# A decoder block with gated recurrence and windowed attention: the attention's two key blocks folded into one block of 128 scores, masks applied behind the turn by VectorE

## The chip, the cores and the metric

One Trainium2 chip (trn2), one of its cores. The metric is the device time of one launch in microseconds (us). The kernel before ran three times: 2208.53 us median, 2208.11 to 2211.46.

## The reference, cut to what matters

One decoder block over 2048 tokens of width 1024: an RMS norm, one input projection, two mixers side by side (a gated linear recurrence with 4 heads, and attention with 8 query heads of 64 on 2 key heads), one output projection, a gated feed-forward part and a last norm. The change lies in the attention:

```python
kk = with_prev(kb)            # keys of the block before and of this block: 256
vv = with_prev(vb)
scores = einsum('bnqhgd,bnshd->bhngqs', qb, kk) * (B_HEAD_DIM ** -0.5)
dist = qi + BLOCK - kj        # 128 queries against 256 keys
valid = ((dist >= 0) & (dist < WINDOW)) & (key_pos >= 0)
scores = where(valid, scores - slopes * dist, -inf)
m = maximum(max(scores), sink)
p = exp(scores - m)
p = p / (sum(p) + exp(sink - m))
o = einsum('bnhgqs,bnshd->bnqhgd', p, vv)
```

WINDOW and BLOCK are both 128. So of the 256 keys beside a query exactly 128 are valid: with query row q and key column k of a block, the key k of this block is valid for k <= q, and the key k of the block before for k > q. The two valid parts fill one 128x128 square without overlap.

## The kernel before, in words

The 2048 tokens go in four blocks (`it`, 0 to 3) of 512. For each block a function `slots(it)` stands in every engine's program, with 27 slots (line 67), and behind it `out_b(it)`; behind all four blocks the feed-forward part (`ffn`, `down`) takes the rest of the time, from about 900 us on. Every engine has its own program and waits for the others by semaphores; the order within an engine is the order in which the code issues.

A slot of TensorE begins with one group: 24 matmuls that make 128 columns of the input projection (`group`, lines 939 to 948). Behind it stand short pieces of the mixers. The attention has 16 steps in a block (4 pairs of heads, `p`, times 4 token tiles, `b`), one per slot, and each step passes through the slots as line 69 says: scores of step i in slot i + 2, probabilities in slot i + 3, the turn in slot i + 4, the product with the values in slot i + 5. Slots 4 to 19 thus hold a turn. In one slot TensorE does, in this order: the group, the turn of a head's output if there is one (line 1083), scores, the turn of the probabilities, the value product, and then the recurrence's pieces.

One step, for two heads (a pair) and 128 queries:

- TensorE (`scores`, line 997): per head two matmuls into 256 columns of bank X[0], which hold the scores against the keys of the tile before and of this tile.
- VectorE (`scores`, lines 1752 to 1763): per head one addition over 256 columns, X[0] plus the slope times a table of distances (`dist`, with a large negative number where a key is not valid; `dist0` for the first tile), into `pr`; one max reduce over 2x256; two small operations for the negative maximum and the sink.
- ScalarE (`scores`, lines 1335 and 1337): two exponentials of 256 columns with their sums, and one for the sink.
- VectorE (`denominators`, lines 1733 and 1737): sum and reciprocal, as the first thing in its next slot.
- GpSimd (`normalise`, line 2306): one product of 128x512 with the two reciprocals. In one step per block it also copies `dist` over `dist0` (line 2311).
- TensorE (`p_turn`, line 1009): four transposes of 128x128 into bank X[1]. It waits for `s_pT` of the step before (line 1005), since the bank is single.
- ScalarE (`p_turn`, line 1343): copies X[1] to `pT`, as the first of the three attention pieces in its slot.
- TensorE (`pv`, line 1020): per head two products of 128 keys with the values, accumulated in M[3].

VectorE's slot (`slots`, from line 1866) holds, in order: the denominators; the low half of the weights for two slots ahead (`make_lo`, line 1704), which waits for ScalarE's high half `whi`, and that for TensorE's group of this slot; the turned head's gate; the low halves of the queries; `scores`; the eviction of four finished value products (line 1899); the head's piece (`head_group`: a scan, gated queries, reciprocals); then `keys` (line 1805), `update` (line 1823, eight in a chain) and `head_sum` (lines 1833 and 1835); and last, in slots 12 to 15 of blocks 1 to 3, the scaling of a row of h (`h_scale`, line 2030).

Before the blocks, GpSimd prepares the tables (lines 2248 to 2278), and TensorE, ScalarE and VectorE wait for its counts INI and DST (line 513).

## Time and profile before

| | |
|---|---|
| median of three runs | 2208.53 us |
| lowest, highest | 2208.11, 2211.46 us |
| the profiled execution | 2210.02 us |
| its span | 2208.3 us |
| mean granted TensorE clock | 0.998 of full speed |
| instructions | 29323 |
| busy: TensorE, VectorE, ScalarE, GpSimd | 2162.4, 1428.7, 1001.3, 455.5 us |

The span is the time from the first to the last instruction of the profiled execution. Names in the profile: PE is TensorE's matmuls, PEld its weight loads, DVE VectorE, ACT ScalarE, POOL GpSimd. L12 is line 12 of the kernel. In a timeline a row gives the start in us, the length in us, engine, line, operation, output and inputs, and how many like it are merged; in square brackets the idle time before it and what ended that.

### The profile page before, as it was taken

The page shows a single profiled execution, that of the slowest core. Times are in us where ns is not written, and L with a number is a line of the kernel's source. Part 1 is how long each engine was busy: PE and PEld are TensorE (multiplying, and loading weights), DVE is VectorE, ACT ScalarE, POOL GpSimd, SP SyncE. Part 2 cuts the span into 40 slices and gives each one's busy share as a digit, 9 for nine tenths or more (in the row PEclk, how much of TensorE's full clock was granted, in tenths as well). Part 3 has the DMA queues.
Part 4 walks back from the last instruction along what each step waited for, and adds up shares of the span by engine and source line. Part 5 has one row for each costly group of instructions (what it writes and reads, how often), then busy time and mean ns, then how long its engine had stood idle before and what let it go on. Part 6 is the DMA issues. An engine that isn't in the chain of part 4 may idle for free.

```text
span 2208.3 us, 29323 instructions
## 1 busy us (share of the span) xinstructions
PE 2162.4 (98%) x10792; PEld 1788.9 (81%) x10792; DVE 1428.7 (65%) x2142; ACT 1001.3 (45%) x1809; POOL 455.5 (21%) x344
## 2 busy tenths in 40 slices
PE   7999999999999999999999999999999999999997
PEld 6887887888888888778888887888888888887886
DVE  5776578657865786867466675568655555554555
ACT  5554465546554554543433333346533333333444
POOL 2231024102320222132232330000223232210000
PEclk9999999999999999999999999999999999999999
DMA  4231432343234314543346566787432323236766
GB/s 125 86 125 60 132 96 85 104 155 96 78 110 157 106 58 127 198 143 122 127 167 221 196 226 206 256 269 261 160 121 85 119 96 119 92 101 233 222 211 214
DMA packets 261534, 323.86 MB, mean 147 GB/s; under 512 B 16400, under 2 KB 167952, under 8 KB 261392
## 3 DMA queue, kind: packets, MB, share of 16 engines
q1 hardware_dynamic: 261392, 321.98, 44.1%
q8 instruction: 87, 1.43, 0.3%
q14 instruction: 55, 0.45, 0.1%
HBM read 244.85 MB, written 77.07 MB: 146 GB/s over the span
## 4 chain that ended last, share of the span: by engine, by line
PE 80%; DVE 8%; issue 6%; ACT 2%; DMA 2%; POOL 1%; SPq 0%; DVEq 0%; ACTq 0%; POOLq 0%
PE M L1193 10%; PE M L1195 10%; PE M L1194 9%; PE M L895 5%; PE M L897 4%; PE M L896 4%; PE M L1219 3%; PE M L1220 3%; PE M L1221 3%; PE X L1220 3%; PE X L1221 3%; PE X L1219 3%; PE X L1195 3%; PE X L1193 3%; PE X L1194 3%
## 5 line engine op out<-in xcount | busy, mean ns | idle before, releaser
L2162 DVE TENSOR_TENSOR ring_lo<-ring_raw,ring_hi 128x1024 fp32r<-128x1024 f32 x154 | 189.3, 1229 | 170.8 <-ACT ring_hi L1607 170.4
L895 PE MATMUL M<-uhi,whi 128*128 128x512 f32 (+1 forms) x720 | 285.6, 397 | 3.7 <-DVE wlo L1704 2.1
L1704 DVE TENSOR_TENSOR wlo<-raw,whi 128x1024 fp32r<-128x1024 f32 x120 | 158.7, 1323 | 190.9 <-ACT whi L1254 190.5
L897 PE MATMUL M<-uhi,wlo 128*128 128x512 f32 (+1 forms) x720 | 278.7, 387 | 0.0
L896 PE MATMUL M<-ulo,whi 128*128 128x512 f32 (+1 forms) x720 | 278.3, 387 | 0.0
L1607 ACT ACTIVATE ring_hi<-ring_raw 128x1024 fp32r<-128x1024 f32 x154 | 163.3, 1060 | 234.5 <-DMA ring_raw<-a_scr 231.2
L1193 PE MATMUL M<-t_hi,wu_hi 128*128 128x512 f32 x616 | 240.2, 390 | 3.5 <-DVE gq L2080 2.6
L1195 PE MATMUL M<-t_hi,wu_lo 128*128 128x512 f32 x616 | 240.0, 390 | 0.0
L1194 PE MATMUL M<-t_lo,wu_hi 128*128 128x512 f32 x616 | 239.7, 389 | 0.0
L1254 ACT ACTIVATE whi<-raw 128x1024 fp32r<-128x1024 f32 x120 | 126.8, 1056 | 189.8 <-PE M L897 113.1
L2048 DVE TENSOR_TENSOR wu_lo<-fraw,wu_hi 128x512 fp32r<-128x512 f32 x132 | 124.5, 951 | 123.0 <-ACT wu_hi L1547 122.6
L2306 POOL TENSOR_TENSOR pr<-pr,rd 128x512 f32<-128x512 f32 x64 | 90.7, 1418 | 506.5 <-DVE rd L1737 506.5
L895 PEld LDWEIGHTS M<-uhi,whi 128*128 128x128 f32 x720 | 136.2, 189 | 35.7 <-issue 7.8
L2362 POOL TENSOR_TENSOR fs<-fraw 128x512 f32<-128x512 f32 x44 | 62.7, 1426 | 470.9 <-DMA fraw<-in_w_gate_dram 210.4
L897 PEld LDWEIGHTS M<-uhi,wlo 128*128 128x128 f32 x720 | 136.3, 189 | 27.9
L896 PEld LDWEIGHTS M<-ulo,whi 128*128 128x128 f32 x720 | 136.5, 190 | 24.4
L1193 PEld LDWEIGHTS M<-t_hi,wu_hi 128*128 128x128 f32 x616 | 115.6, 188 | 28.2 <-DVE wu_lo L2048 4.3
L1194 PEld LDWEIGHTS M<-t_lo,wu_hi 128*128 128x128 f32 x616 | 115.8, 188 | 24.1
L1195 PEld LDWEIGHTS M<-t_hi,wu_lo 128*128 128x128 f32 x616 | 115.6, 188 | 24.1
L2368 POOL TENSOR_TENSOR fraw<-fraw,fs 128x512 f32<-128x512 f32 x44 | 58.6, 1332 | 363.6 <-DVE wl_lo L2048 363.5
L1335 ACT ACTIVATE pr<-pr,nm 128x256 f32<-128x256 f32 x128 | 64.2, 502 | 149.0 <-DVE nms L1763 149.0
L1219 PE MATMUL M<-ring_hi 128*128 128x512 f32 x308 | 120.7, 392 | 5.1 <-DVE ring_lo L2162 5.1
(276 smaller groups left out, 4970.9 us busy)
## 6 DMA issues: line engine op xcount, KB each, us to landing
raw<-in_w_in_dram SPq DMA_DIRECT2D x88, 512.0 KB, 3.9
ring_raw<-a_scr SPq DMA_DIRECT2D x154, 256.0 KB, 3.6
fraw<-in_w_gate_dram SPq DMA_DIRECT2D x44, 512.0 KB, 4.3
fraw<-in_w_up_dram SPq DMA_DIRECT2D x44, 512.0 KB, 4.8
a_scr<-au SPq DMA_DIRECT2D x88, 256.0 KB, 2.4
ring_raw<-t_scr SPq DMA_DIRECT2D x88, 256.0 KB, 3.0
ring_raw<-in_w_down_dram SPq DMA_DIRECT2D x66, 256.0 KB, 3.0
raw<-in_w_out_dram SPq DMA_DIRECT2D x32, 512.0 KB, 3.8
```

The lines of the kernel that those rows point to most:

```text
L895: mm(bank, whi[s][:, kb, :], hi, start=first, stop=False)
L896: mm(bank, whi[s][:, kb, :], lo, start=False, stop=False)
L897: return mm(bank, wlo[s][:, kb, :], hi, start=False, stop=last)
L1193: mm(bank[:, :], wh[:, k, :], hi[:, k, :], start=start and k == 0, stop=False, skip_group_check=True)
L1194: mm(bank[:, :], wh[:, k, :], lo[:, k, :], start=False, stop=False, skip_group_check=True)
L1195: last = mm(bank[:, :], wl[:, k, :], hi[:, k, :], start=False, stop=k == KH - 1, skip_group_check=True)
L1219: mm(banks[b][:, :], hi[:, 1, tokens], hi[:, 0, :], start=first, stop=False, skip_group_check=True)
L1220: mm(banks[b][:, :], hi[:, 1, tokens], lo[:, 0, :], start=False, stop=False, skip_group_check=True)
L1221: done = mm(banks[b][:, :], lo[:, 1, tokens], hi[:, 0, :], start=False, stop=last, skip_group_check=True)
L1607: A(hi[:, :, :], raw_r[:, :, :], ACT.Copy).then_inc(s_rowhi, 1)
L1704: V.tensor_tensor(wlo[s][:, :, :], raw[s][:, :, :], whi[s][:, :, :].bitcast(F32), ALU.subtract).then_inc(s_lo[s], 1)
L2162: V.tensor_tensor(lo[:, :, :], raw_r[:, :, :], hi[:, :, :].bitcast(F32), ALU.subtract).then_inc(s_rowlo, 1)
```

## The change

Both heads' scores stay as they are in X[0]. VectorE first folds: where the key column is at most the query row, the score against this tile's key is copied over the score against the key of the tile before (one predicated copy for both heads, 2x128 columns, within X[0]). The additions, the reduce, the exponentials and the normalisation then run over 128 columns per head instead of 256. TensorE turns one 128x128 square per head, two instead of four. The eviction goes from ScalarE to VectorE: a bitwise AND of the two turned squares with two masks (`parts`), which gives the four squares that the value product takes, in the order (key tile, head) instead of (head, key tile). It stands in VectorE's slot behind `keys`, `update` and `head_sum`, ahead of `h_scale`. The setup makes the new tables; `dist0` lies in the memory of a later tile and is used in block 0 alone, so the copy of `dist` over it goes.

Memory places, the table of semaphore names, and the setup on GpSimd are cut here.

```diff
@@ semaphore counts
-        INI, DST = 9, 4
+        INI, DST = 10, 10
@@ TensorE, p_turn and pv
-                for n in range(4):
+                for n in range(2):
                     last = tr(X[1][:, n * P:(n + 1) * P], pr[i % 2][:, n * P:(n + 1) * P], ident[:, :])
...
-                                  pT[i % 2][:, (2 * par + kb) * P:(2 * par + kb + 1) * P],
+                                  pT[i % 2][:, (2 * kb + par) * P:(2 * kb + par + 1) * P],
@@ ScalarE, scores; p_turn removed
-                    act.wait_ge(s_den, it * STEPS + i)
+                    act.wait_ge(s_den, 2 * (it * STEPS + i) - 1)
                 for par in range(2):
-                    half = pr[w][:, par * 256:(par + 1) * 256]
+                    half = pr[w][:, par * BLOCK:(par + 1) * BLOCK]
...
-            def p_turn(it, i):
-                act.wait_ge(s_ptr, it * STEPS + i + 1)
-                if i >= 2:
-                    act.wait_ge(s_pv, it * STEPS + i - 1)
-                A(pT[i % 2][:, :], X[1][:, :], ACT.Copy).then_inc(s_pT, 1)
...
-                    for begin, step in ((P_TURN, p_turn), (SCORE, scores), (PV, pv)):
+                    for begin, step in ((SCORE, scores), (PV, pv)):
@@ VectorE, parameters
+                V.tensor_copy(parts[:, :, :].bitcast(I32), parts[:, :, :]).then_inc(s_ini2, 1)
@@ VectorE, scores
-                if i == 0 and it:
-                    dve.wait_ge(s_dist, it)
-                d = dist0 if b == 0 else dist
+                d = dist0 if it == 0 and b == 0 else dist
+                both = X[0][:, :].rearrange("p (h k) -> p h k", h=2)
+                V.copy_predicated(both[:, :, 0:BLOCK],
+                                  upto_row[:, :].bitcast(I32).rearrange("p (o k) -> p o k", o=1)
+                                  .broadcast_to([P, 2, BLOCK]), both[:, :, BLOCK:2 * BLOCK]).then_inc(s_fold, 1)
+                dve.wait_ge(s_fold, it * STEPS + i + 1)
                 for par in range(2):
 
                     slope = 2.0 ** -(2 * p + par + 1)
-                    half = slice(par * 256, (par + 1) * 256)
-                    last = V.scalar_tensor_tensor(out=pr[w][:, half], in0=d[:, :], scalar=8.0 * slope,
-                                                  in1=X[0][:, half], op0=ALU.mult, op1=ALU.add)
+                    last = V.scalar_tensor_tensor(out=pr[w][:, par * BLOCK:(par + 1) * BLOCK], in0=d[:, :],
+                                                  scalar=8.0 * slope, in1=both[:, par, 0:BLOCK],
+                                                  op0=ALU.mult, op1=ALU.add)
                 last.then_inc(s_bias, 1)
                 dve.wait_ge(s_bias, it * STEPS + i + 1)
-                V.tensor_reduce(mx[:, :], pr[w][:, :].rearrange("p (h k) -> p h k", h=2), AX_X,
+                V.tensor_reduce(mx[:, :], pr[w][:, 0:2 * BLOCK].rearrange("p (h k) -> p h k", h=2), AX_X,
                                 ALU.max).then_inc(s_mx, 1)
...
+            def p_parts(it, i):
+                dve.wait_ge(s_ptr, it * STEPS + i + 1)
+                if i >= 2:
+                    dve.wait_ge(s_pv, it * STEPS + i - 1)
+                V.tensor_tensor(pT[i % 2][:, :].rearrange("p (k h q) -> p k h q", k=2, h=2).bitcast(I32),
+                                X[1][:, 0:2 * P].rearrange("p (o h q) -> p o h q", o=1, h=2).bitcast(I32)
+                                .broadcast_to([P, 2, 2, P]),
+                                parts[:, :, :].rearrange("p k (o q) -> p k o q", o=1).bitcast(I32)
+                                .broadcast_to([P, 2, 2, P]), ALU.bitwise_and).then_inc(s_pT, 1)
@@ VectorE, slots, behind keys, update and head_sum
                         if a is not None:
                             step(it, a)
+                    i = step_at(slot, P_TURN)
+                    if i is not None:
+                        p_parts(it, i)
                     if slot == SWA_MUL:
@@ GpSimd, normalise
-                pool.wait_ge(s_rd, it * STEPS + i + 1)
-                halves = pr[i % 2][:, :].rearrange("p (h k) -> p h k", h=2)
+                pool.wait_ge(s_den, 2 * (it * STEPS + i) + 2)
+                halves = pr[i % 2][:, 0:2 * BLOCK].rearrange("p (h k) -> p h k", h=2)
                 G.tensor_tensor(halves, halves, rd[:, :].rearrange("p (h o) -> p h o", o=1)
-                                .broadcast_to([P, 2, 2 * BLOCK]), ALU.mult).then_inc(s_prob, 1)
-                if i == (PAIRS - 1) * TB + 1:
-
-                    pool.wait_ge(s_bias, it * STEPS + i)
-                    copy(dist0[:, :], dist[:, :]).then_inc(s_dist, 1)
+                                .broadcast_to([P, 2, BLOCK]), ALU.mult).then_inc(s_prob, 1)
```

## Rows read from the trace of the kernel before

**Rows 1.** The page's first part: busy us (share of the span) and instructions.

```profile
PE 2162.4 (98%) x10792; PEld 1788.9 (81%) x10792; DVE 1428.7 (65%) x2142; ACT 1001.3 (45%) x1809; POOL 455.5 (21%) x344
```

**Rows 2.** Timeline of TensorE at the end of slot 10, block 1: start, length, line, count.

```profile
323.74 0.60 PE L1009 MATMUL X<-ident,pr 128*128 128x128 f32 x4
324.27 0.66 PE L1020 MATMUL M<-pT,vals 128*64 128x128 f32 x8
```

**Rows 3.** Groups of instructions by line: shapes and count, busy us, mean ns, idle before.

```profile
L2306 POOL TENSOR_TENSOR pr<-pr,rd 128x512 f32<-128x512 f32 x64 | 90.7, 1418 | 506.5 <-DVE rd L1737 506.5
L1335 ACT ACTIVATE pr<-pr,nm 128x256 f32<-128x256 f32 x128 | 64.2, 502 | 149.0 <-DVE nms L1763 149.0
L1752 DVE SCALAR_TENSOR_TENSOR pr<-dist,X 128x256 f32<-128x256 f32 x128 | 47.7, 413 | 0.5
L1756 DVE TENSOR_REDUCE mx<-pr 128x2 f32<-128x512 f32 x64 | 43.9, 686 | 2.2
L1009 PE MATMUL X<-ident,pr 128*128 128x128 f32 x256 | 38.3, 272 | 0.0
L1343 ACT ACTIVATE pT<-X 128x512 f32<-128x512 f32 x64 | 37.7, 590 | 0.2
L1805 DVE TENSOR_TENSOR amask<-X,causal 128x512 int32<-128x512 int32 x16 | 10.9, 681 | 0.0
```

**Rows 4.** Timeline of VectorE, the low half of the weights in slots 5 and 10.

```profile
282.81 1.23 DVE L1704 TENSOR_TENSOR wlo<-raw,whi 128x1024 fp32r<-128x1024 f32 x1
...
323.70 1.54 DVE L1704 TENSOR_TENSOR wlo<-raw,whi 128x1024 fp32r<-128x1024 f32 x1 [0.66 <-ACT whi L1254]
```

**Rows 5.** Timeline of VectorE: its first instruction behind slots 4, 8, 10, 13, 15, 16, 18's last.

```profile
282.39 0.13 DVE L1733 TENSOR_TENSOR den<-rs,es 128x2 f32<-128x2 f32 x1
...
314.65 0.15 DVE L1733 TENSOR_TENSOR den<-rs,es 128x2 f32<-128x2 f32 x1
...
331.12 0.15 DVE L1733 TENSOR_TENSOR den<-rs,es 128x2 f32<-128x2 f32 x1
...
355.95 1.28 DVE L2030 SCALAR_TENSOR_TENSOR h<-h,rhln,g2row 128x1024 f32<-128x1024 f32 x1
...
373.68 1.27 DVE L2030 SCALAR_TENSOR_TENSOR h<-h,rhln,g2row 128x1024 f32<-128x1024 f32 x1
...
381.05 0.09 DVE L1733 TENSOR_TENSOR den<-rs,es 128x2 f32<-128x2 f32 x1
...
395.33 2.65 DVE L1823 SCALAR_TENSOR_TENSOR st<-st,cum,X 128x128 f32<-128x128 f32 x7
```

**Rows 6.** Timeline of TensorE: the turns in slots 5, 9, 11, 14, 16, 17, 19.

```profile
281.93 0.60 PE L1009 MATMUL X<-ident,pr 128*128 128x128 f32 x4
...
313.54 0.60 PE L1009 MATMUL X<-ident,pr 128*128 128x128 f32 x4
...
330.97 0.60 PE L1009 MATMUL X<-ident,pr 128*128 128x128 f32 x4
...
355.38 0.60 PE L1009 MATMUL X<-ident,pr 128*128 128x128 f32 x4
...
373.42 0.60 PE L1009 MATMUL X<-ident,pr 128*128 128x128 f32 x4
...
380.62 0.60 PE L1009 MATMUL X<-ident,pr 128*128 128x128 f32 x4
...
398.11 0.60 PE L1009 MATMUL X<-ident,pr 128*128 128x128 f32 x4
```

**Rows 7.** Timeline of TensorE, block 1: two waits of today, in slots 15 and 17.

```profile
365.25 0.66 PE L1083 MATMUL X<-ident,sqo 128*128 128x128 f32 x4 [0.90 <-DVE sqo L1835]
...
382.60 1.16 PE L1045 MATMUL X<-qdec,key 128*128 128x128 f32 x8 [0.79 <-POOL key L2295]
```

**Rows 8.** Timelines of GpSimd and VectorE at the start of the program.

```profile
8.51 0.20 POOL L2276 MEMSET dist<- 128x128 f32 x1
...
24.99 0.15 DVE L1681 TENSOR_TENSOR f_mul<-lbl 128x4 f32<-128x4 f32 x1
```

More of the change, by code:

```diff
@@ L226, in block_program @@
         gu = [at(f"gu{i}", (P, T), gu_at + 2 * K * i) for i in range(2)]
-        dist = at("dist", (P, 2 * BLOCK), dist_at)
-        dist0 = at("dist0", (P, 2 * BLOCK), dist_at + K)
+        dist = at("dist", (P, BLOCK), dist_at)
+        dist0 = at("dist0", (P, BLOCK), mix_at + 22 * K)
+        upto_row = at("upto_row", (P, BLOCK), dist_at + 512)
+        parts = at("parts", (P, 2, BLOCK), dist_at + K)
         causal = at("causal", (P, P), dist_at + 2 * K)
@@ L419, in block_program @@
         s_mx = sem("s_mx")
-        s_nm = sem("s_nm")
+        s_fold = sem("s_fold")
         s_nms = sem("s_nms")
@@ L423, in block_program @@
         s_den = sem("s_den")
-        s_rd = sem("s_rd")
         s_prob = sem("s_prob")
@@ L1697, in parameters @@
                 V.tensor_copy(causal[:, :].bitcast(I32), causal[:, :]).then_inc(s_ini2, 1)
-                dve.wait_ge(s_ini2, 11)
+                V.tensor_copy(parts[:, :, :].bitcast(I32), parts[:, :, :]).then_inc(s_ini2, 1)
+                dve.wait_ge(s_ini2, 12)
             def make_lo(it, n):
@@ L1733, in denominators @@
                 V.tensor_tensor(den[:, :], rs[:, w, :], es[:, :], ALU.add).then_inc(s_den, 1)
-                dve.wait_ge(s_den, it * STEPS + i + 1)
+                dve.wait_ge(s_den, 2 * (it * STEPS + i) + 1)
                 if i:
                     dve.wait_ge(s_prob, it * STEPS + i)
-                V.reciprocal(rd[:, :], den[:, :]).then_inc(s_rd, 1)
+                V.reciprocal(rd[:, :], den[:, :]).then_inc(s_den, 1)
             def scores(it, i):
@@ L2263, in _ @@
                             pattern=[[1, P]], channel_multiplier=-1).then_inc(s_ini, 1)
-            G.tensor_copy(dist0[:, :], dist[:, :].bitcast(I32)).then_inc(s_ini, 1)
+            G.tensor_copy(dist[:, :], dist0[:, :].bitcast(I32)).then_inc(s_ini, 1)
             pool.wait_ge(s_ini, 8)
             G.memset(causal[0:CHUNK, CHUNK:P], 0.0).then_inc(s_ini, 1)
-            G.affine_select(out=dist0[:, :], in_=dist0[:, :], compare_op=ALU.is_ge, fill=MASKED, base=BLOCK,
-                            pattern=[[-1, 2 * BLOCK]], channel_multiplier=1).then_inc(s_dst, 1)
@@ L2271, in _ @@
-            pool.wait_ge(s_dst, 1)
-            G.affine_select(out=dist[:, :], in_=dist0[:, :], compare_op=ALU.is_ge, fill=MASKED, base=-1,
-                            pattern=[[1, 2 * BLOCK]], channel_multiplier=-1).then_inc(s_dst, 1)
+            G.iota(upto_row[:, :].bitcast(I32), [[1, BLOCK]], base=-BLOCK, channel_multiplier=-1).then_inc(s_ini, 1)
+            pool.wait_ge(s_ini, 10)
+            G.affine_select(out=dist0[:, :], in_=dist[:, :], compare_op=ALU.is_ge, fill=0.0, base=0,
+                            pattern=[[-1, BLOCK]], channel_multiplier=1).then_inc(s_dst, 1)
@@ L2274, in _ @@
+            G.tensor_copy(parts[:, 1, :], upto_row[:, :].bitcast(I32)).then_inc(s_dst, 1)
             pool.wait_ge(s_dst, 2)
-            G.tensor_copy(dist0[:, BLOCK:2 * BLOCK], dist[:, BLOCK:2 * BLOCK]).then_inc(s_dst, 1)
-            G.memset(dist0[:, 0:BLOCK], MASKED).then_inc(s_dst, 1)
+            G.affine_select(out=parts[:, 1, :], in_=parts[:, 1, :], compare_op=ALU.is_ge, fill=0.0, base=-1,
+                            pattern=[[1, BLOCK]], channel_multiplier=-1).then_inc(s_dst, 1)
+            pool.wait_ge(s_dst, 3)
@@ L2277, in _ @@
+            G.tensor_tensor(dist[:, :], dist0[:, :], parts[:, 1, :], ALU.add).then_inc(s_dst, 1)
             pool.wait_ge(s_dst, 4)
-            pool.wait_ge(s_ini, 9)
+            G.memset(upto_row[:, :], -1.0).then_inc(s_dst, 1)
+            G.memset(parts[:, :, :], -1.0).then_inc(s_dst, 1)
+            G.affine_select(out=dist0[:, :], in_=dist[:, :], compare_op=ALU.is_ge, fill=MASKED, base=0,
+                            pattern=[[-1, BLOCK]], channel_multiplier=1).then_inc(s_dst, 1)
+            pool.wait_ge(s_dst, 7)
@@ new lines, in _ @@
+            G.affine_select(out=upto_row[:, :], in_=upto_row[:, :], compare_op=ALU.is_ge, fill=0.0, base=0,
+                            pattern=[[-1, BLOCK]], channel_multiplier=1).then_inc(s_dst, 1)
+            G.affine_select(out=parts[:, 0, :], in_=parts[:, 0, :], compare_op=ALU.is_ge, fill=0.0, base=-1,
+                            pattern=[[-1, BLOCK]], channel_multiplier=1).then_inc(s_dst, 1)
+            G.affine_select(out=parts[:, 1, :], in_=parts[:, 1, :], compare_op=ALU.is_ge, fill=0.0, base=0,
+                            pattern=[[1, BLOCK]], channel_multiplier=-1).then_inc(s_dst, 1)
@@ L2280, in copy @@
+            pool.wait_ge(s_dst, 10)
             def copy(out, in_):
```

9 lines of the change are left out of this document (4 added, 5 removed).

## The prediction, made before the changed kernel had run

> **What bounds the kernel now.** I read the page's first part before anything else: TensorE is busy 98% of the span, VectorE 65%, ScalarE 45%, GpSimd 21% [rows 1], and the table of times has the mean granted clock at 0.998 of its upper level, 2.4 GHz. So TensorE's stream of work sets the end, and any time that TensorE loses or saves in it moves the end one for one. Where little idle time is left, two questions remain for a change: how much TensorE work it takes away, and whether it makes TensorE wait for something that today comes earlier.
>
> The change touches the 64 attention steps (4 token blocks of 16). One slot is one 24-matmul projection group and then short work: scores of step i, turn of step i-2, product with V of step i-3. The timeline of TensorE shows the turn: four 128x128 transposes start at 323.74 and the V product follows at 324.27 [rows 2]. They take 0.53 us of the stream, 0.1325 each, though a record of one says 272 ns [rows 3]: they overlap.
>
> **What it takes from TensorE.** Two of four transposes in each of 64 steps: 64 x 0.265 = 17.0 us. The score matmuls and the eight V passes keep their number and shape.
>
> **What it takes from ScalarE and GpSimd.** ScalarE loses the 0.59 us eviction of the turned block and half the width of two exponentials of 0.50 [rows 3]; it isn't the bound, so I cost this at nothing, except that the exponentials end about 0.5 us sooner after VectorE's last score operation. GpSimd's product goes from 512 to 256 columns, from 1.4 us mean today [rows 3]; its result is needed only behind the next slot's group of 24 matmuls, so also nothing. One effect counts: where VectorE's low half of the weights runs beside that product it takes 1.54 instead of 1.23 us [rows 4]. In slots 4 and 10 of a block I give VectorE those 0.31 us back.
>
> **What it does to VectorE in its score part.** Today: two biased additions of 0.41 us, a reduce of 0.69 [rows 3]. Halving the width takes 128 elements off each addition and 256 off the reduce. From 0.69 us at 512 elements against 0.41 at 256, 256 elements cost 0.27, so this saves 0.27 + 0.27 = 0.54. The added predicated copy is not in the trace. Its nearest row is the 256-wide addition that reads the same bank: 0.41, plus 0.04 for the wait behind it, 0.45. Net -0.09 us a step. From below, if it moved two elements a cycle, it would cost 0.41 less half of the 0.27 that 256 elements take, 0.28; a gain is excluded, since it is work that wasn't there. From above as much as the 512-wide PSUM operation, 0.68 [rows 3], net +0.18.
>
> **What it adds at the end of VectorE's slot.** The eviction with both masks is an AND of a 128x512 PSUM operand with a broadcast mask, the form of line 1805: 0.68 us [rows 3]; for VectorE's own queue I take 0.60, an estimate, since operations that don't depend on each other overlap a little. It stands behind everything that VectorE does in the slot (scores, scan, reciprocals, the eight state updates) except the scaling of h (line 2030), which comes behind it. And TensorE's next turn, in the next slot, waits for it (line 1005), since both use bank X[1]; the V product behind it waits too, and in TensorE's in-order stream so does the next group. Today ScalarE does the eviction early in its slot and nobody waits.
>
> So the price is read thus: the AND would start where VectorE's next instruction starts today, TensorE can go on 0.74 us later (0.68 and 0.06 of release), and that is set against the start of its next turn. For block 1, VectorE's starts [rows 5] and TensorE's [rows 6]:
> slot 4: 282.39 + 0.74 - 281.93 = 1.20 late;
> slot 8: 314.65 + 0.74 - 313.54 = 1.85;
> slot 10: 331.12 + 0.74 - 330.97 = 0.89;
> slot 13: 355.95 + 0.74 - 355.38 = 1.31;
> slot 15: 373.68 + 0.74 - 373.42 = 1.00;
> slot 16: 381.05 + 0.74 - 380.62 = 1.17;
> slot 18: 397.9 (the end of the updates) + 0.74 - 398.11 = 0.53.
> In the other slots the same difference is at most 0.33 (slot 5), mostly far below zero.
>
> These aren't simply added. Most of VectorE's slots begin with a wait for whi, made right behind TensorE's group, so TensorE's lateness L carries over to VectorE; each turn between gives back 0.265. Walking through block 1, L at the next turn:
> slot 4: 1.20 - 0.09 - 0.31 = 0.80. Three turns later (slots 5 to 7), at the end of group 8: 0.01.
> slot 8: 0.01 - 0.09 + 1.85 = 1.77; end of group 10: 1.51.
> slot 10: 1.51 - 0.09 - 0.31 + 0.89 = 2.00; two turns more, end of group 13: 1.47.
> slot 13: 1.47 - 0.09 + 1.31 = 2.69; end of group 15: 2.43. VectorE enters slot 14 with a backlog, but loses it there, where today it waits for a root that ScalarE makes behind the exponentials. TensorE's present idle 0.90 before the head's turn [rows 7] is filled: 1.53, then 1.27 at group 16.
> slot 15: VectorE starts 2.00 late (backlog 0.60 behind slot 14), ends 1.91 late: 1.91 + 1.00 = 2.91.
> slot 16: backlog again 2.51, less 0.09 and about 0.30 of relief: 2.12 + 1.17 = 3.29. TensorE's present wait of 0.79 for the keys [rows 7] is filled: 2.23 at group 18.
> slot 18: 2.23 + 0.53 = 2.76, less the last turn's 0.265: 2.5 us.
> So a block loses 8.4 us in waits, gets back 1.7 of today's idle time, saves 4.24 in transposes (8.4 - 1.7 - 4.2 = 2.5), and ends 2.5 us later. Blocks 2 and 3 repeat the pattern. Block 0 has no scaling of h and so not the two idle times of 0.90 and 0.79; with them left out it ends about 4 us later. Sum: 4 + 3 x 2.5 = **+11.5 us**.
>
> **Setup.** GpSimd prepares more masks. Its old ones end at 8.7, VectorE asks for them at 25.0 [rows 8]; some ten more short operations of 0.2 to 0.4 us end before 14. One 256-wide cast on VectorE falls into its wait for whi behind. Nothing. The copies of one distance table into the other, one per block on GpSimd, go: nothing.
>
> **The number.** The profiled execution took 2210.0 us (span 2208.3), 1.5 above the median of the three, 2208.5. The sum is on the span's account; added to the median it gives 2220.0. Bounds: the predicated copy at 0.68 adds 0.27 in six or seven slots of four blocks, +7; at 0.28 it takes 3; no relief from GpSimd's shorter product +3; an AND that costs only 0.60, -2. The case's own range is 2213 to 2231.
>
> **Rivals.**
> *The parts are ready in time (faster).* The only place is the end of VectorE's slots 4, 8, 10, 13, 15, 16 and 18. If VectorE reached these ends over 1.2 us sooner (by GpSimd's contention falling away everywhere, not only in two slots), TensorE would wait nowhere and the 17.0 us show: 2191.5. For it: the low half takes up to 0.3 too long in several slots. Against: slot 8, the worst, runs without contention and would still be 1.85 late. It decides where the differences above fall below zero. 0.09.
> *Waits and savings cancel.* Each wait is about 0.45 smaller than worked out (28 x 0.45 = 12.6), since TensorE's own lateness gives VectorE room that I don't credit: 2207 to 2209. 0.14.
> *The predicated copy is dear.* PSUM to PSUM with a mask, it takes 1.23 us like a 1024-wide operation: +0.82 in six or seven slots of four blocks, some +20: 2240. 0.06.
> *Transposes cost more of the stream than their spacing says.* Each at its recorded 272 ns would give 128 x 0.272 = 35 us instead of 17, 18 us less than my sum: 2202, faster. The spacing in [rows 2] speaks against it. 0.03. The Trainium skill, "TensorE: Matmul & The Clock Gate", Part 4 (PE-mode transpose), gives about 275 ns for a transpose within a kernel, limited by access latency; the record's 272 ns agrees, but four in 0.53 us show that here the latency is overlapped.
>
> **Chances.** My forecast has 0.68. About 0.2% (4.4 us) is what a measurement of this kernel can tell from no change. Slower by more: 0.68 + 0.06 = 0.74. Within: most of the cancelling case, 0.13. Faster: 0.09 + 0.03 + a remainder 0.01 = 0.13. The range takes in the cancelling case and the bounds upward, 2204 to 2232; outside are the two faster cases and the dear copy.
>
> **What the profile after should show.** Half as many transposes of the probabilities (128 for 256), turns of 0.27 us; TensorE idle some 28 to 36 us in the 64 steps, put down to VectorE's AND, in slots 4, 8, 10, 13, 15, 16 and 18, longest behind slot 8 (about 1.9 us); VectorE busy some 30 us more (64 x 0.6 less 64 x 0.09), ScalarE some 65 us less (64 x 0.59 and 128 x 0.23); GpSimd's product near 0.6 to 0.8 us. I'm wrong if TensorE's waits for the AND sum to under 17 us (then it is faster), if the predicated copy takes over 0.7 us, or if TensorE loses time outside the 64 steps.

## The result, and the profile after

The changed kernel takes 2228.19 us, the median of four runs (2224.96 to 2231.32); the kernel before took 2209.28 beside it (four runs, 2208.11 to 2211.46). The ratio is 1.0082, with a 95% interval of 1.007 to 1.0094: slower, by about 18 us by the ratio and 18.9 by the medians. The profiled execution is the 2225.45 one, with a span of 2223.7 us, 15.4 more than the span before.

The first part of the page answers to [rows 1]: busy us, share of the span and instructions of each engine.

```profile
PE 2154.0 (97%) x10664; PEld 1777.1 (80%) x10664; DVE 1456.7 (66%) x2271; ACT 957.6 (43%) x1745; POOL 421.2 (19%) x347
```

TensorE has less to do and takes longer: 128 transposes are gone and its share fell from 98 to 97%. VectorE has 28.0 us more, ScalarE 43.7 less, GpSimd 34.3 less.

The groups by line of the changed kernel, for [rows 3]: shapes and count, busy us, mean ns, idle before. L1770 is the AND, L1745 the predicated copy, L2334 GpSimd's product, L1338 the exponentials, L1752 and L1757 the additions and the reduce, L1012 the turn.

```profile
L2334 POOL TENSOR_TENSOR pr<-pr,rd 128x256 f32<-128x256 f32 x64 | 67.3, 1052 | 539.5 <-DVE rd L1735 539.5
L1338 ACT ACTIVATE pr<-pr,nm 128x128 f32<-128x128 f32 x128 | 50.5, 395 | 173.1 <-DVE nms L1764 173.1
L1770 DVE TENSOR_TENSOR pT<-X,parts 128x512 int32<-128x512 int32 x64 | 42.6, 665 | 0.0
L1752 DVE SCALAR_TENSOR_TENSOR pr<-dist,X 128x128 f32<-128x128 f32 x128 | 31.0, 283 | 2.2
L1745 DVE COPY_PREDICATED X<-upto_row,X 128x256 f32<-128x256 int32 x64 | 27.0, 422 | 0.5
L1757 DVE TENSOR_REDUCE mx<-pr 128x2 f32<-128x256 f32 x64 | 26.9, 420 | 2.2
L1012 PE MATMUL X<-ident,pr 128*128 128x128 f32 x128 | 25.1, 278 | 29.8 <-DVE pT L1770 29.8
```

The last row has the finding: 29.8 us of idle time on TensorE, ended by the AND. The view of waits has the same from TensorE's side. First the changed kernel's waits of TensorE from 20 to 930 us (the four blocks): waiting group, releaser, us in total, times, the longest.

```profile
PE X L1012 <- DVE pT L1770: 29.8, 24, 1.9
PE X L1048 <- POOL key L2323: 3.0, 4, 1.1
PE M L897 <- DVE wlo L1702: 2.1, 1, 2.1
PE X L1072 <- DVE st L1834: 1.8, 4, 0.8
```

The same view of the kernel before, from 20 to 900 us:

```profile
PE X L1045 <- POOL key L2295: 5.4, 7, 1.0
PE X L1083 <- DVE sqo L1835: 3.7, 7, 0.9
PE M L895 <- DVE wlo L1704: 2.1, 1, 2.1
PE X L1069 <- DVE st L1823: 1.8, 4, 0.8
```

The new wait is six a block (24 in all). Of the old ones, the wait for `sqo` is gone and the wait for the keys has shrunk: 5.4 + 3.7 - 3.0 = 6.1 us of idle time came back, since TensorE now arrives there later.

The timeline of TensorE in block 1 of the changed kernel: the turns in slots 5, 9, 11, 14, 16 and 19, which answer to [rows 6]. In the slot before each of them VectorE made the AND too late. The turn in slot 17, which [rows 6] also has, does not wait.

```profile
284.82 0.41 PE L1012 MATMUL X<-ident,pr 128*128 128x128 f32 x2 [0.69 <-DVE pT L1770]
...
317.65 0.41 PE L1012 MATMUL X<-ident,pr 128*128 128x128 f32 x2 [1.93 <-DVE pT L1770]
...
337.10 0.41 PE L1012 MATMUL X<-ident,pr 128*128 128x128 f32 x2 [1.16 <-DVE pT L1770]
...
362.40 0.41 PE L1012 MATMUL X<-ident,pr 128*128 128x128 f32 x2 [1.38 <-DVE pT L1770]
...
380.98 0.41 PE L1012 MATMUL X<-ident,pr 128*128 128x128 f32 x2 [1.67 <-DVE pT L1770]
...
405.19 0.41 PE L1012 MATMUL X<-ident,pr 128*128 128x128 f32 x2 [0.67 <-DVE pT L1770]
```

The worst place closer up, the end of slot 8 on VectorE: the AND has its input long before, but stands behind the chain of state updates.

```profile
314.25 2.65 DVE L1834 SCALAR_TENSOR_TENSOR st<-st,cum,X 128x128 f32<-128x128 f32 x7
316.82 0.68 DVE L1770 TENSOR_TENSOR pT<-X,parts 128x512 int32<-128x512 int32 x1
317.42 0.15 DVE L1731 TENSOR_TENSOR den<-rs,es 128x2 f32<-128x2 f32 x1
```

And TensorE at the same time (the second row stands in the list above as well; here are the scores before it and the V product behind it):

```profile
315.07 0.64 PE L999 MATMUL X<-kk,qs 128*128 128x256 f32 x4
...
317.99 0.67 PE L1023 MATMUL M<-pT,vals 128*64 128x128 f32 x8
```

The scores start at 315.07 and the turn at 317.65, 2.58 later. Where nothing waits, the turn can start 0.49 behind the scores (e6 below has both rows). 2.58 - 0.49 = 2.09, and the row shows an idle time of 1.93: the stream loses 0.16 us more than the idle time. Behind slot 15 (scores at 378.66, turn at 380.98, idle 1.67) it is 2.32 - 0.49 - 1.67 = 0.16 again, and so for all 20 waiting turns that stand directly behind the scores: start to start less the idle time is 0.64 in each. The V product also follows a turn that waited 0.34 later (317.65, 317.99), where it follows another 0.31 later (the rows of slot 15 below). Together a wait costs 0.19 us beyond its idle time.

The clock, too, answers. The view by windows of the changed kernel, around that wait: window, length, TensorE busy (count), granted clock, DMA share, GB/s.

```profile
316.00:319.00 3.00, 1.35 (x12) 0.96 0.01 5
319.00:322.40 3.40, 3.40 (x25) 0.53 0.56 161
322.40:326.00 3.60, 3.60 (x16) 1.00 0.00 0
```

TensorE had been idle for 1.93 us; about 1.1 us after it started again (the 0.96 of the first window puts the fall 0.24 us before 319.0) it got half its clock, the 1.2 GHz level, for 3.4 us, and the upper level of 2.4 GHz behind that. Half speed for 3.4 us costs 1.7 us of work. Leaving out the program's end, the changed kernel's profile has three such stretches (at 318.8, 779.6 and 2011.8), the one of before a single one (at 190.6, behind a wait of 1.04 us for the keys); the changed kernel's first two lie behind the wait of slot 8 in blocks 1 and 3, the third in the feed-forward part.

**Where the 15.4 us come from**, in one account of the two profiled executions: +29.8 of waits for the AND; -6.1 of old idle time filled; +4.6 for starting again (24 x 0.19); +3.4 for two more stretches at the lower level; -14.1 for the transposes (below); -0.6 at the start of the program (the first scores come at 38.48 instead of 39.11). Sum 17.0, against 15.4 measured. Ten of the 18 old waits are gone, and the cost of starting again behind them with them; at the same 0.19 each, an estimate, that is 1.9 less, and the sum 15.1. At the first scores of blocks 1, 2 and 3 TensorE is 2.29, 6.85 and 9.97 us later than before, at slot 19 of block 3 14.69, at the end 15.4. So nearly all is lost in the 64 steps; behind them the stretch at 2011.8 costs 1.7, and small gains of about 1 us hide most of it. Block 2, in which neither profile has a stretch at the lower level, gets 3.1 us later.

**What a turn costs.** A turn that doesn't wait, in the timeline of TensorE of the changed kernel (slot 15, block 1):

```profile
372.17 0.38 PE L1012 MATMUL X<-ident,pr 128*128 128x128 f32 x2
372.48 0.66 PE L1023 MATMUL M<-pT,vals 128*64 128x128 f32 x8
```

Two transposes take 0.31 us of the stream, where four took 0.53 [rows 2]: the last two of the four cost 0.11 each, less than the first two. So a step saves 0.22, and 64 save 14.1 us, not 17.0.

### The profile page after: what moved, and what is told of

The parts are those of the page before. It is cut to its first block, busy times and chain, and to the rows that moved or that the text cites. A ratio compares the mean times of both kernels' runs of the same rounds, so it can differ in the third digit from the quotient of the medians.

```text
span 2223.7 us, 29130 instructions
## 1 busy us (share of the span) xinstructions
PE 2154.0 (97%) x10664; PEld 1777.1 (80%) x10664; DVE 1456.7 (66%) x2271; ACT 957.6 (43%) x1745; POOL 421.2 (19%) x347
## 4 chain that ended last, share of the span: by engine, by line
PE 77%; DVE 11%; issue 6%; ACT 3%; DMA 2%; POOL 1%; SPq 0%; DVEq 0%; ACTq 0%; POOLq 0%
PE M L1196 9%; PE M L1198 9%; PE M L1197 9%; PE M L897 4%; PE M L899 4%; PE M L898 4%; PE M L1222 3%; PE M L1223 3%; PE M L1224 3%; PE X L1223 3%; PE X L1222 3%; PE X L1224 3%; PE X L1198 3%; PE X L1197 3%; PE X L1196 3%
## 5 line engine op out<-in xcount | busy, mean ns | idle before, releaser
L1702 DVE TENSOR_TENSOR wlo<-raw,whi 128x1024 fp32r<-128x1024 f32 x120 | 154.1, 1284 | 175.6 <-ACT whi L1257 175.4
L2334 POOL TENSOR_TENSOR pr<-pr,rd 128x256 f32<-128x256 f32 x64 | 67.3, 1052 | 539.5 <-DVE rd L1735 539.5
L1338 ACT ACTIVATE pr<-pr,nm 128x128 f32<-128x128 f32 x128 | 50.5, 395 | 173.1 <-DVE nms L1764 173.1
```

What stands on the lines that cost most here:

```text
L1702: V.tensor_tensor(wlo[s][:, :, :], raw[s][:, :, :], whi[s][:, :, :].bitcast(F32), ALU.subtract).then_inc(s_lo[s], 1)
```

## The experiments

The theory behind them: the time goes where the AND stands, at the end of VectorE's slot, while TensorE waits for bank X[1]. Rivals: the fold's own work loads VectorE, wherever the AND stands; the masks or the AND's form is what costs; the removal of transposes saves less, or more, than assumed. Medians in us; ratios are to the kernel before in the same session, whose medians were 2211.0 to 2211.7 (2210.1 for e12).

| kernel | median | ratio, 95% interval | TensorE waits for the AND (or eviction) |
|---|---|---|---|
| the change again (e11) | 2227.4 | 1.0072 [1.0059, 1.0086] | 29.8, 24 times |
| e1, AND behind the scores | 2210.5 | 1.0001 [0.9992, 1.001] | none |
| e2, eviction by ScalarE, no masks | 2194.53 | 0.9925 [0.9912, 0.9939] | none |
| e3, four transposes | 2233.97 | 1.0107 [1.0092, 1.0123] | 24.6, 24 times |
| e4, only the place, in the kernel before | 2239.48 | 1.0129 [1.0116, 1.0143] | 30.4, 27 times |
| e5, AND behind the queries' low half | 2210.53 | 0.9999 [0.999, 1.0008] | 9.6, 12 times |
| e6, e1 and the scaling of h spread | 2203.44 | 0.9964 [0.9951, 0.9977] | none |
| e7, the scaling spread, in the kernel before | 2207.61 | 0.9987 [0.9978, 0.9997] | none |
| e8, the predicated copy twice | 2253.9 | 1.0194 [1.0181, 1.0207] | 41.1, 27 times |
| e9, e1 and the scaling in slots 12 and 17 | 2195.96 | 0.9929 [0.9916, 0.9943] | none |
| e10, AND early in slot 8 alone | 2218.64 | 1.0034 [1.0021, 1.0046] | 22.1, 20 times |
| e12, e9's scaling in the kernel before | 2205.66 | 0.9983 [0.9974, 0.9992] | none |

### e4: the place alone

The kernel before, with four transposes and 256 columns, and its plain copy of X[1] moved from ScalarE to the place where the change has the AND:

```diff
-                A(pT[i % 2][:, :], X[1][:, :], ACT.Copy).then_inc(s_pT, 1)
+                V.tensor_copy(pT[i % 2][:, :], X[1][:, :]).then_inc(s_pT, 1)
```

> The kernel before with one thing moved: the eviction of the turned block (128x512, a plain copy) goes from ScalarE to VectorE's slot, at the place that it has in the changed kernel. No fold, no shorter operations, four transposes. Theory (the place): TensorE waits for it in the same slots, 4, 8, 10, 13, 15, 16 and 18, about 30 us in all (26 to 35), with nothing saved against it, some 6 us of it taking the place of today's idle time: 2209.3 + 26, 2230 to 2242. Rival (the waits come from the fold's longer dependency chain, not from the place): under 5 us of waits and 2209 to 2214.

It is 28.5 us slower than the kernel before. TensorE's waits in e4, same columns as above:

```profile
PE X L1009 <- DVE pT L1764: 30.4, 27, 1.8
PE X L1045 <- POOL key L2299: 3.0, 4, 1.1
```

Of the old waits again 6.1 us are gone. 30.4 - 6.1 + 27 x 0.19 = 29.4, against 28.5 by the medians and 29.5 by the spans. (The sum leaves out that e4's profile has three stretches at the lower level to the one of before, +3.4 at most, and ten old waits less to start again behind, -1.9 by the estimate above.) The fold and the masks have no part in the loss: the place by itself costs more than the whole change, and what the change saves elsewhere brings it down.

### e3: four transposes again

The changed kernel, but the two squares are turned twice, the second time for nothing:

```diff
-                for n in range(2):
-                    last = tr(X[1][:, n * P:(n + 1) * P], pr[i % 2][:, n * P:(n + 1) * P], ident[:, :])
+                for n in range(4):
+                    last = tr(X[1][:, n * P:(n + 1) * P], pr[i % 2][:, n % 2 * P:(n % 2 + 1) * P], ident[:, :])
```

> The changed kernel with four transposes in each turn again (two of them turn the same squares once more, into columns that nobody reads), all else as changed. If a transpose costs what its spacing says (0.1325 us), TensorE's stream gets 17.0 us longer, but VectorE gets 0.265 us more per slot before its end is met, so the waits of 29.8 us shrink by some 8: the time rises by 7 to 11 us over the changed kernel, to about 2237. If each transpose cost its recorded 278 ns, it would rise by over 20, to 2250 or more. If the saving were wholly covered by the waits, it would rise by under 3.

The spans give +6.4 us (2230.1 against 2223.7), the medians +5.8 against the change's first 2228.19 and +6.6 against e11. Of the 14.1 us the waits take up a part, since TensorE comes later to them: 24.6 instead of 29.8, 5.2. That leaves 8.9. The profile of e3 also has two stretches at the lower clock level, where the changed kernel's has three, which takes off another 1.7: 7.2, against the 6.4 of the spans. The rise lies just under the 7 to 11 us that were expected. In any case two transposes a step are not worth 18 us more than the spacing says: the rival that priced each at its recorded 272 ns falls.

### e2: ScalarE evicts, nobody masks

The eviction goes back to ScalarE, in its old place; the two masks are left out, so the V product takes every folded probability with the values of both tiles:

```diff
+            def p_turn(it, i):
...
+                A(pT[i % 2][:, :].rearrange("p (k h q) -> p k h q", k=2, h=2),
+                  X[1][:, 0:2 * P].rearrange("p (o h q) -> p o h q", o=1, h=2).broadcast_to([P, 2, 2, P]),
+                  ACT.Copy).then_inc(s_pT, 1)
```

> The eviction goes back to ScalarE at its old place, as a 128x512 copy of the two turned squares, without the masks (the masks are left out of the computation); VectorE keeps the fold. Theory: no wait of TensorE for the eviction is left, VectorE loses 64 x 0.6 = 38 us of work: 2188 to 2193, the price that the change would have if the masked eviction cost nothing. Rival (the predicated copy and its wait hold TensorE up through the scores): the time stays above 2200, with waits of TensorE for VectorE's additions.

2194.5: with the eviction off VectorE the fold saves what its transposes promise. The old waits stay as they were (4.8 for the keys, 3.8 for `sqo`, 1.9 for the state: 10.5, against 10.9 before), and the spans differ by 16.2 us (2208.3 - 2192.1), where 14.1 + 0.6 + 0.4 = 15.1 are accounted for. So the fold's score part (copy, additions, reduce) adds nothing to TensorE's time.

### e1: the AND behind the scores

The AND as in the change, but directly behind `scores` in VectorE's slot, ahead of the head's piece, the keys and the updates:

```diff
                     i = step_at(slot, SCORE)
                     if i is not None:
                         scores(it, i)
+                    i = step_at(slot, P_TURN)
+                    if i is not None:
+                        p_parts(it, i)
...
-                    i = step_at(slot, P_TURN)
-                    if i is not None:
-                        p_parts(it, i)
```

> The masked eviction moves in VectorE's slot from behind the head's work to directly behind the score part; nothing else changes. Theory (the place): TensorE's 29.8 us of waits for it fall to under 2 us, the next turn finds its bank free a whole group earlier, and the 17.0 us of saved transposes show: 2209.3 - 17 = 2192, between 2188 and 2197 by what becomes of the smaller waits of today (TensorE for the turned head and for the keys, some 13 us in the kernel before). Rival (the load: VectorE's slots have become too long, wherever the eviction stands): waits of like size turn up elsewhere in TensorE's stream, for the low halves of the weights, the head's turn or the keys, and the time stays at 2220 to 2230.

All 24 waits for the AND are gone and 17 to 18 us with them, but not the 30 or more expected: the kernel ties with the one before. TensorE's waits in e1:

```profile
PE X L1048 <- POOL key L2323: 11.8, 8, 2.9
PE X L1086 <- DVE sqo L1846: 5.3, 8, 1.4
PE X L1072 <- DVE st L1834: 4.9, 11, 0.8
```

22.0 us, against 10.9 in the kernel before: the old waits grew by 11.1. The longest of them is in slot 17. VectorE's reciprocal there, GpSimd's product for the keys and TensorE's matmul, from the three timelines of e1, block 1:

```profile
375.38 1.74 DVE L1804 RECIPROCAL cuminv<-cum 128x256 f32<-128x256 f32 x1
...
377.26 2.34 POOL L2323 TENSOR_TENSOR key<-key,cuminv 128x512 f32<-128x512 f32 x1 [3.25 <-DVE cuminv L1804]
...
379.66 2.08 PE L1048 MATMUL X<-qdec,key 128*128 128x128 f32 x8 [2.85 <-POOL key L2323]
```

The clock over the end of that wait and behind it, by windows of e1:

```profile
376.00:380.00 4.00, 1.15 (x11) 0.87 0.63 240
380.00:384.00 4.00, 4.00 (x16) 0.50 0.42 123
```

Stretches at the lower level make up 13.7 us of e1's profile ahead of the program's end, against 3.4 before, which costs another 5.1 us. (That execution, 2213.46 us, is one of e1's slower ones.)

In slots 12 to 15 of blocks 1 to 3 VectorE also scales a row of h (1.27 us each). From the end of slot 13 to slot 17 it has no idle time but its wait for a root; whatever the fold adds to it comes out at the next thing that TensorE needs, here `cuminv`. So the rival of VectorE's load was right in one place: in the last slots of the scaling the load counts, elsewhere the order.

### e5: the AND one piece later

Behind the scores, the four finished products and the head's low halves of the queries, but still ahead of keys, updates and `head_sum`:

```diff
                     if mul is not None:
                         head_lo(it, mul)
+                    i = step_at(slot, P_TURN)
+                    if i is not None:
+                        p_parts(it, i)
```

> The masked eviction stands one place earlier than in the changed kernel: behind head_group and head_lo, but ahead of keys, the eight state updates and head_sum. By the place theory only the slots whose length lies in those pieces are relieved: 8, 13 and 18 (1.9, 1.3 and 0.5 us late per block), and TensorE no longer comes late out of them, so slots 4, 10, 15 and 16 keep about 1 us each: TensorE's waits for it fall from 29.8 to 12 to 18 us, and the time to 2209 to 2217. If it isn't the eviction's place but VectorE's load, nothing changes against 2228; if only being behind the score part matters, it equals the run with the eviction there, 2210.5 with under 2 us of waits for it.

2210.5, the same as e1 and within the range expected. Of the waits for the AND 9.6 us in 12 places stay, less than the 12 to 18 expected: three a block, ahead of the turns in slots 5, 11 and 16. But `cuminv` is now made ahead of the AND, and the keys' wait is back at 3.0. With the 5.4 for `sqo` and 4.3 for the state it comes to 22.3 us, where e1 had 22.0. Waits have been exchanged for others, which points to VectorE's queue, not to a particular operation.

### e6, e7: the load taken out of the dense slots

e6 is e1 with the scaling of h spread: one row each in slots 12 and 13, two in 17. e7 is the same move in the kernel before, to see what it is worth without the fold.

```diff
-                    if it and 0 <= slot - H_SCALE < TB:
-                        h_scale(it - 1, slot - H_SCALE)
+                    if it:
+                        for c in {12: (0,), 13: (1,), 17: (2, 3)}.get(slot, ()):
+                            h_scale(it - 1, c)
```

> The eviction directly behind the score part, and the scaling of h (1.2 us each on VectorE) of slots 14 and 15 moved to slot 17, so that VectorE has 2.4 us less to do ahead of the reciprocal in slot 16 that GpSimd's keys wait for. With the eviction there TensorE waited 11.8 us for the keys, up to 2.9 at once in slot 17, and its clock fell behind that. Theory (the load piles up in slots 13 to 16 alone): the waits for the keys fall back to 3 to 5 us, and the 17 us of saved transposes show at last: 2190 to 2199, faster than both kernels. Rival (the load piles up everywhere): 2205 to 2210.

> The kernel before with nothing but the scaling of h of slots 14 and 15 moved to slot 17: what that move is worth by itself. In blocks 1 to 3 TensorE's idle time of 0.90 us (slot 15) and 0.79 (slot 17) should go: 3 x 1.7 = 5 us, 2203 to 2208. If the move matters only beside the eviction, it stays within 2 us of the kernel before.

e7 gains 0.13% (interval 0.03 to 0.22%), in the range expected, but by half of what was expected to go: the keys' wait fell from 5.4 to 3.0 and the one for `sqo` stayed at 3.7. e6 gains 7 us on e1, less than expected. In it the keys' wait fell from 11.8 to 6.3, the one for `sqo` stayed at 5.3. TensorE's timeline of e6 in slots 15 and 17 of block 1, with the scores and the turn between them:

```profile
360.23 0.66 PE L1086 MATMUL X<-ident,sqo 128*128 128x128 f32 x4 [1.43 <-DVE sqo L1846]
...
374.66 0.65 PE L999 MATMUL X<-kk,qs 128*128 128x256 f32 x4
375.15 0.38 PE L1012 MATMUL X<-ident,pr 128*128 128x128 f32 x2
...
377.15 1.16 PE L1048 MATMUL X<-qdec,key 128*128 128x128 f32 x8 [1.03 <-POOL key L2324]
```

The row of h in slot 13 still stands ahead of what `sqo` needs.

### e9, e12: the scaling in slots 12 and 17

So the rows were put into slots 12 (two) and 17 (two), again with the AND behind the scores (e9), and in the kernel before as a control (e12):

```diff
-                        for c in {12: (0,), 13: (1,), 17: (2, 3)}.get(slot, ()):
+                        for c in {12: (0, 1), 17: (2, 3)}.get(slot, ()):
```

> The eviction behind the score part everywhere, and the scaling of h in slots 12 (two of four) and 17 (two), so that slot 13's goes too. In the run with slots 12, 13 and 17 TensorE still waited 1.43 us for the turned head in slot 15 and 1.03 for the keys in slot 17, both behind VectorE's backlog out of slot 13. If that backlog is their cause, 1 us of each goes in blocks 1 to 3, 4 to 6 us: 2197 to 2200. If the 0.6 us of the eviction in the slots 14 to 16 themselves is, it stays at 2203.

> The kernel before with the scaling of h in slots 12 (two) and 17 (two) and nothing else, the control of the fastest version. If that version's gain of 15.7 us is mostly the saved transposes (14 us by the spacing of 0.31 us for a turn of two against 0.53 for four), this kernel gains only the idle times of slots 15 and 17, 3 to 6 us: 2205 to 2208. If the move of the scaling makes the gain, it comes to 2200 or below.

e9 is the fastest, 0.71% under the kernel before and 31 us under the changed kernel. TensorE's waits in e9:

```profile
PE X L1072 <- DVE st L1834: 4.4, 8, 0.8
PE X L1048 <- POOL key L2324: 4.1, 8, 1.0
PE X L1086 <- DVE sqo L1846: 1.8, 8, 0.2
```

10.3 us, about the 10.9 of before, so the saving of the transposes shows whole: its span is 2194.2, 14.1 less than before, and the account has -14.1 - 0.6 - 0.6 = -15.3, and +1.7 since its profile has two stretches at the lower level, both behind the attention's blocks, to the one of before: -13.6. e12 shows that the scaling's place alone is worth 0.17% (interval 0.08 to 0.26%); the other 0.54%, some 12 us, needs the fold.

### e10: early in slot 8 alone

The AND goes behind the scores in slot 8, the slot with the longest wait, and stays at the end in all others:

```diff
+                    i = step_at(slot, P_TURN)
+                    if i is not None and slot == 8:
+                        p_parts(it, i)
...
-                    if i is not None:
+                    if i is not None and slot != 8:
                         p_parts(it, i)
```

> The changed kernel with the eviction behind the score part in slot 8 alone, at its place behind the head's work in all other slots. In the changed kernel the longest waits (1.9 us) come from slot 8, and in its profile the granted clock is at its lower level for 3.4 us behind two of them. Theory (place, and the clock behind long waits): TensorE's waits for the eviction fall from 29.8 to about 21 us, the time by 6.6 us for that and by 3 or more for falls of the clock that don't come: 2216 to 2221. Rival (the falls have nothing to do with these waits): the time falls by 6 to 7 us alone and the mean clock stays at 0.994 to 0.996.

8.8 us less than e11 in the same session, for four waits of 1.9 (7.7 us; 22.1 against 29.8 in sum). The waits alone don't make that: the one for the state rose from 1.8 to 4.4 and 0.9 for `sqo` came, so that in sum only 4.2 us of waiting are gone. The profile of e10 has no stretch at the lower level in the attention's blocks and one in all, where the changed kernel's has three, which cost 3.4 us more: 4.2 + 3.4 + 4 x 0.19 = 8.4, and the spans differ by 8.5 (2223.7 - 2215.2). The mean clocks of its five runs are 0.995 to 0.998, those of e11 0.994 to 0.996. Only the AND of slot 8 was moved. And in e11's profile three stretches at the lower level lie in the attention's blocks, each from 0.5 to 1.6 us behind the end of slot 8's wait, in blocks 0, 1 and 3; e3's two lie behind that wait in blocks 0 and 2. So the lower clock goes with the wait, though not with every one.

### e8: the predicated copy twice

```diff
+                for again in range(2):
...
-                dve.wait_ge(s_fold, it * STEPS + i + 1)
+                    dve.wait_ge(s_fold, 2 * (it * STEPS + i) + again + 1)
```

> The changed kernel with the predicated copy made twice in each step (the second copies the same values again). It costs VectorE 0.46 us more ahead of the eviction. If the copy lies on the path that sets the waits in six or seven slots per block, the time rises by 0.46 x 6.5 x 4 = 12 us (10 to 15), and TensorE's waits for the eviction from 29.8 to about 42. If it is covered, it rises by under 3.

25.7 us over the changed kernel, twice what was expected. The waits are as expected, 11.3 us more. First TensorE's waits for the AND in e8, then its clock over the attention's blocks, by windows:

```profile
PE X L1012 <- DVE pT L1771: 41.1, 27, 2.4
```

```profile
35.00:930.00 895.00, 847.71 (x4794) 0.98 0.33 100
```

The same window of the changed kernel:

```profile
35.00:930.00 895.00, 859.51 (x4919) 1.00 0.35 108
```

The mean clock of the whole execution fell from 0.996 to 0.988, and its profile has 12 stretches at the lower level ahead of the program's end, one of them of 6.8 us: 44.4 us in all, where the changed kernel's three make 10.2. At half speed that costs 17.1 us more. 11.3 of waits, 17.1 of clock and 3 x 0.19 for three more waits make 29.0, and the spans differ by 28.3 (2252.0 - 2223.7). The expectation left the clock out, which is the larger part. The copy's own price, 0.42 us, holds.

### e11: the changed kernel again

> The changed kernel once more, beside the two below on one chip. Its four runs fell into two at 2225 us (granted clock 0.996 and 0.997) and two at 2231 (0.994). If the clock's falls behind TensorE's waits make that difference, the runs again order by their mean clock, about 2 us for each 0.001; if they don't, time and clock are unrelated.

Five runs, 2224.92 to 2230.92, and the same 29.8 us in 24 waits. Over these and the first four runs the time rises by about 2.2 us for each 0.001 that the mean clock is lower (0.994 to 0.997), if not in strict order: the slowest of the five has 0.995, the next 0.994. That is no trait of the changed kernel alone: the kernel before scattered by 7 to 8 us within each session (2206.14 to 2213.39 in the first).

## Why the prediction was right, and where its terms were off

Forecast 2220.0 [2204, 2232], slower; measured 2228.19. Against the median of before that it started from, 2208.53, +11.5 forecast and +19.7 measured; +18.9 against 2209.28, and +15.4 by the profiled spans. The direction and the mechanism held; the size came out short, by terms that were mis-sized or missing. That it came out no shorter is in part luck: the waits were taken 4 us too long, which made up for as much of what the sum left out. The range as stated, 2213 to 2231 for this case, is also a little wider than the bounds named, which from 2220.0 give 2215 (-3 and -2) to 2230 (+7 and +3).

- **TensorE waits for the AND behind seven slots.** Right for six. The walk gives for block 1, slot by slot (the lateness after a slot, less what it would be without its wait): 1.07, 2.03, 0.76, 1.49, 1.65, 0.65, 0.79 behind slots 4, 8, 10, 13, 15, 16, 18. Measured: 0.69, 1.93, 1.16, 1.38, 1.67, none, 0.67. In sum 8.4 against 7.5 a block; for all blocks about 34 against 29.8. Slot 16's wait was the smallest in the walk, and didn't come.
- **The transposes give back 17.0.** Here the step "two of four transposes ... 64 x 0.265" failed: it took half of four for the price of two. Two take 0.31 of four's 0.53, so 14.1. The Trainium skill, "TensorE: Matmul & The Clock Gate", Part 4 (PE-mode transpose), gives about 275 ns for the duration of a transpose within a kernel, most of it access latency; the record's mean of 278 ns agrees with the figure. What the stream pays is another thing: 0.31 for two and 0.11 for each of two more, neither 275 ns each nor a fixed 0.1325.
- **Today's idle time comes back, 1.7 a block in blocks 1 to 3.** 5.1 forecast, 6.1 measured.
- **Missing: the cost of starting again.** The sum took a wait at its idle time. Each cost 0.19 us more, 4.6 us in all, of which the old waits that went give some back.
- **Missing: the clock.** The sum had TensorE at its upper level throughout. Two more stretches of 3.4 us at 1.2 GHz in the profiled execution cost 3.4 us; by the mean clocks, 0.996 in it and 0.994 in two of its other runs, more in those. e10 and e8 support this term: their spans come out with it to 0.1 and 0.7 us, and not without it.
- **VectorE's pieces.** The predicated copy 0.42 us (taken 0.41, bounds 0.28 and 0.68), the AND 0.67 (0.68), additions 0.28 and reduce 0.42, VectorE +28.0 us (+30): right. The relief of 0.31 in slots 4 and 10 came too: the low half of the weights there takes 1.22 us (279.11 and 329.24 in VectorE's timeline of the changed kernel) instead of 1.54.
- **ScalarE and GpSimd cost nothing.** Right for the time, wrong for the sizes. An exponential went from 0.50 to 0.395 us, not to 0.27; ScalarE -43.7, not -65. GpSimd's product was forecast at 0.6 to 0.8; its median is 0.62, its mean 1.05 (last section).
- **Loss only within the 64 steps.** Right but for 1.7 us of the clock in the feed-forward part; 14.69 of the 15.4 us are there at slot 19 of block 3.

The rivals. *Ready in time* falls with the 24 waits; e1 shows that it needs another place and, for the last slots of the scaling, less load. *Waits and savings cancel*: what the waits take off was 4 us less than forecast, not 12.6. *The predicated copy is dear* falls with 0.42 us, and with e8, in which its doubling adds 11.3 us of waits, near the 12 that 0.46 us each was expected to add. *Transposes at 272 ns each* falls with the 0.31 and e3.

**Not settled:** what decides which wait is followed by the lower level (slot 8's of 1.93 us is in blocks 1 and 3 of the profile, but not in blocks 0 and 2; in the kernel before a wait of 1.04 is). The 10 us of waits that e9 still has, for the state, the keys and `sqo`, weren't tried.

## What to carry to other kernels

Where a helper engine frees a buffer of the bounding engine, the piece belongs where its input is ready, not at the end of the helper's slot: the same AND cost 30 us of waits there and none behind the scores. Then look at what the earlier piece pushes back in the helper's densest slots, since the gain showed only when the load there was moved as well (e1 to e9, 14.5 us). Price a wait of the bounding engine at its idle time plus the restart and, behind some, a stretch at the lower clock; and price a shorter batch of pipelined instructions from its own spacing, not as a share of the longer one.

## What the runs showed of the hardware that was not expected

**Half the columns made GpSimd's product short only where VectorE left it alone.** The median went from 1.04 to 0.62 us, but the mean only from 1.42 to 1.05. The source view of that line in the changed kernel, with minimum, median and maximum in ns:

```profile
L2334 POOL TENSOR_TENSOR pr<-pr,rd x64: 613/616/1598, 43.4 to 855.3; 128x256 f32<-128x256 f32 x64
```

One of the long ones, in slot 9 of block 1, with VectorE's low half of the weights beside it, from the two timelines of the changed kernel:

```profile
317.69 1.22 DVE L1702 TENSOR_TENSOR wlo<-raw,whi 128x1024 fp32r<-128x1024 f32 x1
...
317.85 1.53 POOL L2334 TENSOR_TENSOR pr<-pr,rd 128x256 f32<-128x256 f32 x1 [12.01 <-DVE rd L1735]
```

VectorE's operation ends at 318.91, GpSimd's at 319.38, 0.47 later, though it had started at 317.85: most of its 0.61 us of work lay behind VectorE's end. The reverse, in slot 7, where GpSimd was first, again from the timelines of the changed kernel:

```profile
297.86 1.29 POOL L2323 TENSOR_TENSOR key<-key,cuminv 128x512 f32<-128x512 f32 x1 [4.59 <-DVE cuminv L1804]
...
298.18 0.99 DVE L1731 TENSOR_TENSOR den<-rs,es 128x2 f32<-128x2 f32 x1
```

A sum of two columns, elsewhere 0.15 us, takes 0.99 and ends at 299.17, with GpSimd's product (299.15). The Trainium skill, "SBUF — State Buffer", in its section "SBUF: two separate sides", says that VectorE and GpSimd share a pair of ports under an exclusive lock: whoever starts first has it for the whole instruction, and the other is blocked. For a VectorE operation outside its two-port modes this holds if it has two inputs in SBUF, as both of these have, and the GpSimd operation reads SBUF. The second pair of rows agrees to 0.02 us, the first to 0.14 (the lock would have the product end at 318.91 + 0.61 = 319.52, and it ended at 319.38). So in such pairs a short operation of the one costs what is left of a long one of the other.

**Idle time is not the whole price of a wait**: 0.19 us more behind each of the 20 waits that were measured, and another 1.7 us behind some, through the clock. It didn't take a long wait: stretches at the lower level began behind waits of 1.93 us in the changed kernel and of 1.04 us in the one before. In a kernel whose bounding engine runs at 98% this makes the difference between the waits and their cost.
